# SyncE's order within a pair of cache loads: value group before key group

## What is computed

```python
s = jnp.concatenate([jnp.einsum('bqhd,bkhd->bhqk', q, k_past), ...], axis=-1) * scale
logits = jnp.where(kpos[None, :] <= qpos[:, None], s + bias, -jnp.inf)
p = jax.nn.softmax(logits, axis=-1)
return jnp.einsum('bhqk,bkhd->bqhd', p[..., :p_len], v_past) + ...
```

## Time and profile before

| | |
|---|---|
| median of 3 runs | 2175.74 us (2175.48 to 2181.7) |
| the profiled execution | 2178.27 us, of which 2176.5 us lie between its first and last instruction |
| busy share of the span | PE 92%, PE weight load 86%, DVE 53%, ACT 30%, POOL 10% |
| the stretch of the change | 376 us (first key copies) to 1076 us (last value group) |
| bytes read from memory | 247.77 MB, of which the cache is 512 copies of 256 KB, all from SP |
| mean granted TensorE clock | 0.961 of full speed |

### The profile page before, as it was taken

The page is one execution under the profiler, slowest core; times in us unless marked ns, Lnnn a source line. Parts: engine busy times, 40 slices in busy tenths (PEclk is TensorE's granted clock), DMA queues, the critical chain, the costliest instruction groups (busy, mean ns, idle before and its releaser), DMA issues.

```text
span 2176.5 us, 39095 instructions
## 1 busy us (share of the span) xinstructions
PE 1999.7 (92%) x14335; PEld 1868.4 (86%) x14335; DVE 1158.6 (53%) x1771; ACT 647.7 (30%) x1178; POOL 216.3 (10%) x253
## 2 busy tenths in 40 slices
PE   7998998898899799799798999799999999999996
PEld 5896887887798698698688898699999999999996
DVE  3654454967856866876332865733322333233348
ACT  4444443134123123223311101444301332123224
POOL 1000000020010020020000100400000001000004
PEclk9998999999899899899889999899999999999999
DMA  3211102597887877787742411111111111111154
GB/s 119 67 36 44 39 20 92 191 315 248 272 296 248 267 263 269 258 291 240 229 147 94 121 49 29 30 48 39 49 48 49 48 39 49 48 49 39 42 150 129
DMA packets 152256, 277.55 MB, mean 128 GB/s; under 512 B 19105, under 2 KB 58398, under 8 KB 152118
## 3 DMA queue, kind: packets, MB, share of 16 engines
q1 hardware_dynamic: 116114, 175.78, 24.3%
q0 software_dynamic: 23232, 82.80, 12.9%
q10 hardware_dynamic: 12800, 17.40, 2.2%
HBM read 247.77 MB, written 28.25 MB: 127 GB/s over the span
## 4 chain that ended last, share of the span: by engine, by line
PE 43%; DVE 5%; DMA 1%; issue 1%; ACT 1%; DVEq 0%; SPq 0%; ACTq 0%
PE bank L121 39%; PE bank L1624 3%; DVE x_lo L1845 1%; DMA gated_raw<-gated_t_scratch 1%; DVE chunk_tmp L1774 0%; DVE chunk_tmp L1776 0%; DVE z L1842 0%; PE banks L1582 0%; DVE merged_hi L1778 0%; DVE moving_lo L1780 0%; DVE w_lo L1915 0%; DMA tail_raw<-in_w_down_dram 0%; DVE y L1891 0%; DMA z<-fox_t_scratch 0%; PE banks L1610 0%
## 5 line engine op out<-in xcount | busy, mean ns | idle before, releaser
L121 PE MATMUL bank<-x_hi,w_hi 128*128 128x344 f32 (+1 forms) x1944 | 642.6, 331 | 55.1 <-DVE rot_sin L1267 25.2
L121 PE MATMUL bank<-x_lo,w_hi 128*128 128x344 f32 (+1 forms) x1944 | 632.2, 325 | 0.0
L121 PE MATMUL bank<-x_hi,w_lo 128*128 128x344 f32 (+1 forms) x1944 | 631.9, 325 | 0.0
L121 PEld LDWEIGHTS bank<-x_hi,w_hi 128*128 128x128 f32 (+1 forms) x1944 | 373.0, 192 | 73.7 <-issue 62.9
L121 PEld LDWEIGHTS bank<-x_lo,w_hi 128*128 128x128 f32 (+1 forms) x1944 | 372.8, 192 | 1.6
L121 PEld LDWEIGHTS bank<-x_hi,w_lo 128*128 128x128 f32 (+1 forms) x1944 | 372.7, 192 | 1.7
L97 ACT ACTIVATE w_hi<-w_raw 128x1024 fp32r<-128x1024 f32 (+3 forms) x139 | 141.7, 1022 | 550.1 <-PE bank L121 372.4
L121 PE MATMUL bank<-moving_hi,w_hi 128*128 128x344 f32 x744 | 229.8, 331 | 25.8 <-DVE moving_lo L1756 14.1
L121 PE MATMUL bank<-moving_lo,w_hi 128*128 128x344 f32 x744 | 239.6, 322 | 0.0
L104 DVE TENSOR_TENSOR w_lo<-w_raw,w_hi 128x1024 fp32r<-128x1024 f32 (+3 forms) x139 | 164.4, 1183 | 117.1 <-ACT w_hi L97 115.8
L121 PE MATMUL bank<-moving_hi,w_lo 128*128 128x344 f32 x648 | 210.0, 324 | 0.0
(11 more groups left out here) (270 smaller groups left out, 2782.5 us busy)
## 6 DMA issues: line engine op xcount, KB each, us to landing
cache_keys<-in_cache_k_dram SPq DMA_DIRECT2D x256, 256.0 KB, 4.6
cache_vals<-in_cache_v_dram SPq DMA_DIRECT2D x256, 256.0 KB, 5.0
w_raw<-in_w_in_dram POOLq DMA_DIRECT2D x52, 512.0 KB, 5.6
w_raw<-in_w_up_dram POOLq DMA_DIRECT2D x22, 512.0 KB, 4.5
w_raw<-in_w_gate_dram POOLq DMA_DIRECT2D x22, 512.0 KB, 4.5
tail_raw<-in_w_down_dram SPq DMA_DIRECT2D x22, 448.0 KB, 3.9
gate<-gate_t_scratch SPq DMA_DIRECT2D x16, 516.0 KB, 3.5
w_raw<-in_w_down_dram POOLq DMA_DIRECT2D x10, 448.0 KB, 4.4
```

Of the source, the lines that this page charges most:

```text
L121: mm = pe.matmul(g.bank[n][0:m, 0:TC], w[slot][:, k, 0:m], x[:, k, chunk(n)], start=(k == 0 and i == 0), stop=(k == kt - 1 and i == 2))
```

## The change

In `period`, the two calls for a slot change places: SP first waits for the value buffer and issues the two value copies of sample n, then waits for the key buffer and issues the two key copies of sample n + 1. Nothing is added or removed. The keys of sample 0 and the values of sample 7 are issued by loops of their own, which stay.

```diff
                     with sp.Fori(0, NG // SLOTS) as q:
                         key_ids, value_ids = page_ids(n + 1, q), page_ids(n, q)
                         for slot in range(SLOTS):
+                            load_group(vals, v_land, v_used, cv, n, q, slot, value_ids)
                             load_group(keys, k_land, k_used, ck, n + 1, q, slot, key_ids)
-                            load_group(vals, v_land, v_used, cv, n, q, slot, value_ids)
```

## The result

The changed kernel takes 2192.97 us in the median of four runs (2191.75 to 2193.92), the kernel before 2177.51 us in four (2175.48 to 2181.7). The ratio is 1.0072, with a 95% interval of 1.0054 to 1.0090: 15.5 us slower, where 4.7 us had been forecast, and outside the range. (The forecast was counted from 2175.74 us, the median of the first three of the four.) The profiled execution took 2191.75 us, with a span of 2189.8 us; that of before had 2176.5, so the two profiles differ by 13.3 us in the span.

What follows compares the result with a forecast made beforehand. PE, busy for 92% of the span, was taken to bound the kernel. The terms 3 x (2.8 - 0.1) - 1.0 - 2.4 = +4.7 us took the median from 2175.74 to 2180.4 us, range 2171 to 2190.

Steps and rivals of the forecast that it cites:

- Part 1: Odd periods: V4 early, its 4.16 us wait removed, nothing gained by it; rotation waits grow from 18.4 to some 30 us.
- Part 2: First rotation of the odd periods: DVE's shift is between -0.7 and +1.0 us for a period, taken as -0.1.
- Part 3: End of odd periods: K12 and K15 late behind value buffers, PE waits 2.0 and 0.8 us, 2.8 us each period.
- Rival (c): End of odd periods: loop from value buffer to rotation decides, landing takes 6 us; +12.5 us, 2188.2 us; chance 0.26.
- Its sign for a full queue: SP's issues in the odd periods take 1.50 and 2.09 us where most take 0.85: queue full at times.
- Rival (a): Waits for values simply go, the whole 22.3 us, giving 2153.4 us; chance 0.07.
- rival (b): End of odd periods is covered, K12 and K15 land in time: -3.7 us, 2172.0 us; chance 0.17.
- Part 4: Periods 2 and 4: K8 and K9 about 3 us later, covered by DVE's 7.32 us of idle time; nothing.
- Parts 5 and 6: Period 0: earlier values, -1.0 us (bounds -1.8 and +0.7); period 6: shorter value waits, -2.4 us (bounds -4.3 and +1).

Runs made afterwards that it cites:

- e2: Kernel before, with values first only in the last round (groups 12 to 15) of the odd periods: 2192.11 us, ratio 1.0067.
- e3: Changed kernel plus 16 matrix products of no use on PE ahead of the third product of each odd period: 2188.22 us, ratio 1.0046.
- e6: Kernel before, with DVE taking K9 to K15 of the odd periods one step later, SP's order untouched: 2169.54 us, ratio 0.9972.
- e1: Changed kernel, with the old order in the last round (groups 12 to 15) of the odd periods alone: 2175.26 us, ratio 0.9987.
- e9: Changed kernel, SP's order untouched, with PE taking values of the odd periods earlier, V8 to V10 in its long wait: 2166.36 us, ratio 0.9961.
- e12: The changed kernel itself run once more, on the chip of e9: 2190.80 us, ratio 1.0065 to the kernel before.
- e7: e1 plus 74 matrix products of no use on PE ahead of the second product of each odd period: 2173.25 us, ratio 0.9978.

## Why the prediction was wrong, point by point

**Part 1** was right. V4 went out at 527, ahead of K4, its wait is gone in all three odd periods (in period 5 a wait of 1.33 us for V5 is new), and nothing was won by it. The size of the wait that took its place was too small: the first rotations' waits, without the new ones, are 39.1 us (13.46, 13.76, 11.84), where "some 30" stood. The V4 waits had stretches at half clock behind them (3.4, 6.8 and 6.8 us), which went too; PE was at the rotation earlier by that as well, and stood there longer. This was the first sign of the omission below.

**Part 2** was right for period 1: the first product behind the rotation began at 566.68 in place of 567.49, of which 0.6 us are the earlier start of the period; -0.2 us, where -0.1 was taken. Counted from V0 in the same way, period 3 has +0.3 (40.84 us in place of 40.56) and period 5 +1.25 (40.33 in place of 39.08), which is beyond the bound of +1.0: there K8 landed 5.8 us after the round's first issue, where it had been 3.4. In sum +1.3 us, where -0.3 was taken.

**Part 3** is the step that failed, by a term that it had at nothing: the clock behind the new waits. Its mechanism, its place and its first wait were right: K12 out at 575.36 (575.34 forecast), landed by 579.44 (580.0), a wait of 2.27 us (2.0). That the two agree so well is in part luck, since K12 landed 4.1 us after its issue and not 4.7, and PE wanted the bank 0.7 us earlier. The second wait was 1.70 us in period 1, not 0.8: SP's issue of V15 took 2.00 us, which had been in the text as the bound, 0.5 to 1.7, and not as the value taken; in periods 3 and 5 it was 1.05 and 0.50. The clock was missing altogether. The sum counted a wait of PE as the time of the wait. Behind four of the six new waits it is 1.7 us more, because the clock then falls to half for 3.4 us.

Measured, the odd periods cost 18.9 us; parts 2 and 3 had 8.1. The rows give these terms:

| term | forecast | profile |
|---|---|---|
| three waits for the second rotation | 6.0 | 7.0 (46.1 - 39.1) |
| three waits for `w_lo` | 2.4 | 3.3 |
| clock behind these waits, 4 x 1.7 | 0 | 6.8 |
| first rotation reached later | -0.3 | +1.3 |
| clock behind the first rotation, period 3 | 0 | +0.9 |

The last line is that behind the first rotation of period 3 PE works 5.7 us at half clock, where it was 4.0. Together 19.3, against 18.9. So the clock is the largest part of the error, and the size of the waits a small one. That the stretches belong to the waits is shown by e2 and e3; why some waits have one behind them and others none stays open.

The rows of before could have told it. After PE's wait for V4 they show a granted clock of one half, for 3.4 us in period 1 and 6.8 in periods 3 and 5:

```profile
544.60:548.00 3.40, 3.40 (x12) 3.40 (x13) 2.27 (x4) 0.00 (x0) 0.00 (x0) 0.50 1.01 354
718.70:725.50 6.80, 6.07 (x34) 5.51 (x35) 5.68 (x7) 0.00 (x0) 0.00 (x0) 0.50 1.03 384
```

I had seen them, and had also seen that the waits of 2.66 and 2.18 us in period 0 had none behind them, and left the clock out with no term and no bound. A bound of 1.7 us for each of six waits, 10 us, would have put the end of the range at 2200, and the measured time inside.

**Rival (c)** had the right sign and place for the right reason, and the wrong lever: it put its price on a slower landing, 6 us, when K12 landed in 4.1 us and K15 in 4.8, against the 4.7 taken. K14 did take 6.3, and PE did not wait for it. Its sign for a full queue, SP's slow issues, is not shown by any run; what sets their length stays open. **Rival (a)** is refuted by the table of waits, **rival (b)** by the new waits.

**Part 4** had the right mechanism. DVE waits for K8 and K9 in period 2 were there, 4.21 and 0.93 us; K9 was 4.2 us later, not 3, and the idle time ahead of the `w_lo` covered it (7.32 us in the earlier trace rows, 3.16 now). Yet periods 2 and 4 are longer by 1.1 and 1.5 us. Both have a wait of PE for DVE's `dec_out` (line 930, 1.3 us) that the kernel before has at 0.3 to 0.4. But e6, where SP has the old order throughout, has it too, with 1.16 us in its period 2. And the periods differ as much with one order: period 2 lasts 83.5 us in e2 and 84.8 in e6, where the even periods have the old order in both. So neither the wait nor the 1.1 and 1.5 us can be put down to the change, and what sets them stays open.

**Parts 5 and 6**: -0.6 with the earlier start (forecast -1.0), and -2.5 (forecast -2.4). What I had at nothing, the values of sample 7 and the work behind, was 5.1 us shorter; the wait for V9 there fell from 3.39 to 1.13 us. Its loop was not changed, and this is no effect of the order that could be shown: the same stretch lasts 1134.6 us in e2 (old order in the even periods) and 1138.7 in e1 (new order), as if the two had changed places. The same holds for period 0 (85.8 us in e6 and 87.5 in e2, both with the old order). Period 6 lasts 75.4 and 76.3 us in e2 and e6, and 72.5 to 77.6 in the ten profiles with the new order there beside the changed kernel's own; its -2.5 is likely but small against this.

In sum: forecast +4.7; odd periods +10.8 more, periods 2 and 4 +2.6, period 0 +0.4, period 6 -0.1, the end -5.1; the profiles' +13.3. Only that of the odd periods is more than the scatter between profiles.

## What to carry to other kernels

When two streams of loads share one in-order issuer, ask which stream's buffer the issuer will wait for, and what then stands behind it: here the same swap cost 0.67% in one round of three periods (e2) and nothing that could be told in all the others (e1). Put first the one whose buffer is free first, which may change from one stage to the next, or make the consumer give the buffer back before the issuer asks (e9). And a short wait of PE is to be priced with the clock that follows it: look in the profile of before at what stands behind waits of the same size, and give the term bounds even where you hold it for nothing.

## What the runs showed of the hardware

Two waits of TensorE of 2.27 and 1.70 us in period 1 of the changed kernel were each followed within 0.5 us by 3.4 us at 1.2 GHz, while waits of 2.66 and 2.18 us in period 0 of the kernel before had full clock around them (1.00 over all of 440.4 to 526.7 us). So the length of a wait alone doesn't tell. At the two places of the new waits, in the profiles of the changed kernel, e2 and e12, all twelve waits of 1.70 to 2.92 us had such a stretch behind them, and the six of 0.21 to 1.33 us had none.

In e3 the clock stayed at 1.00 over the 33 us from 571 us on, once the first wait was filled with 16 products of no use. The Trainium skill says (TensorE: Matmul & The Clock Gate, Part 1: The HAM clock gate) that the slow clock is the resting state and that TensorE's own activity is what lifts it. By that rule filling the wait is what should help the clock. The traces of e3 and e7 agree: with the filler the clock was 1.00 where it had been 0.90 and 0.91. What they don't show is the time that one would expect from it: e7's median was 2 us lower than e1's, where 9 were expected.

A key group behind a value group landed 4.1 us (K12), 4.8 us (K15) and 6.3 us (K14, beside a weight load) after its issue in period 1 of the changed kernel, where the first of a round (K8 in the kernel before) took 3.4. From V12's issue to K12's landing, 1 MB in all, 5.96 us went by; the prediction's rows had 5.8.
